# Retention heads: chunks of 128 tokens with carried states, and state products inside the head's last projection

## The chip, the cores and the metric

The kernel runs on one NeuronCore of one Trainium2 chip. The metric is device time in microseconds (us), of which less is better. Engines are named as in the profile: PE is TensorE's matmul side and PEld its weight load, DVE is VectorE, ACT is ScalarE, POOL is GpSimd, SP is SyncE, which here only issues DMAs. "L936" is line 936 of the kernel.

## What is computed

One step of a one-layer decoder whose mixer has two halves, eight heads of sparse attention and eight heads of retention, for a prompt of 512 tokens and for 8 samples of one token each (520 columns in all). The retention half, cut to what matters:

```python
def ret_chunk(R, q, k, v, lg):                      # RET_CHUNK = 128, dk = dv = 128
    decay = where(i - j >= 0, exp((i - j) * lg), 0)
    inner = einsum('bhij,bjhe->bihe', einsum('bihd,bjhd->bhij', q, k) * decay, v)
    cross = einsum('bihd,bhde->bihe', q, R) * exp((i + 1) * lg)
    zeta  = exp((n - 1 - i) * lg)
    R_new = exp(n * lg) * R + einsum('bjhd,bjhe,jh->bhde', k, v, zeta)
    return R_new, inner + cross
# prompt: lax.scan over 4 chunks from R = 0; samples: one step from a given state (8 x 8 x 128 x 128)
# then ret_o * rsqrt(mean(ret_o^2) + eps) * silu(gate), next to the attention half, @ w_out, MLP
```

Outputs are the two results, the new keys and values, and the retention states of the prompt and of the samples.

## The kernel before, in words

Activations lie in SBUF with features on partitions and the 520 tokens on the free side. Each projection is in "tiles": one tile makes 128 output features for 520 tokens, by two units of 8 contraction steps. Weights and activations are split into a high and a low part, so a step has three products (high by high, high by low, low by high), each for two halves of 260 tokens: 48 matmuls a unit, 96 a tile (`unit` and `tile`, L647). SP loads a unit's weights to one of two raw buffers, ACT makes the high part in a ring of four, POOL the low part from it.

The part that is changed is a loop over 8 heads. One round makes attention head i and retention head i. PE's order in a round is written out by hand: four tiles (values, queries, keys, gate of the retention head), and between their units or behind them the small products of both heads. All of these go through four PSUM banks `B`. The product groups of a round are numbered; `fill(e)` on PE waits until the group three before e has been taken out, DVE's `full(e)` waits until group e is there. DVE takes every group out, in order; the semaphore `s_xd` counts this.

In a round before the change:

- between the units of the second tile (`values_and_scores`): values turned, attention scores (groups 0 to 5)
- behind the third tile: the attention probabilities turned (groups 6 to 9)
- between the units of the fourth tile (`output_and_decay`): the attention output (group 10), the retention scores of each block of 128 keys with all later queries, 512, 384, 256 and 128 columns (groups 11 to 14, from `rk` and `rq`), the keys turned (15 and 16). DVE multiplies the scores by the decay `dh` to `sd_h` (L1713), makes `ktok` (turned keys by zeta, L1716), `ks_tok` and `vbd` (samples' keys and values in split form, L1657 to L1719)
- behind the fourth tile, "the tail": samples' key-value products (17 and 18, which DVE adds to the decayed states `rs`, L1725), the retention output from `sd_h` and `vtok_r` by 512, 384, 256 and 128 columns (19), the prompt's state from `ktok` and `vtok_r` (20), the samples' outputs, eight products of one column with `rs` (21). DVE copies the output to `ro`, ACT squares it to `rv`, PE sums the squares with a matrix `ones` (22 for the prompt, 23 for the samples), DVE takes the sums out.

Then DVE and ACT form the root, its inverse (L1432 to L1436) and the gated product into `mix` (L1741), beside the next round's first tile. SP waits for this before it loads the next `dh`, `rs` and a weight unit. In the last round ACT also copies `mix` to the input of the output projection (`mixed`, L1156), before and between its squares; POOL (L605) and DVE (L1747) form the low parts, step by step as that projection asks for them.

The core of the code before, in the tail:

Of the kernel before, what the change touches and what calls it, by code (L numbers as in the profile page):

```python
# [14 lines left out]
P = 128  # L15
D = 2048
KT = D // P
NP_, NS = 512, 8
T = NP_ + NS
# [42 lines left out]
def unit_of(tile):  # L62

    return 2 * tile
# [59 lines left out]
def build(nc, x_prompt, x_sample, cache_k, cache_v, cache_idx_k, state_ret, page_table, norm1_g, w_in,  # L124
# [3 lines left out]
    with ctx:  # L128
# [109 lines left out]
        sd_h = at("sd_h", H0, [P, 1280])  # L238
# [90 lines left out]
        def pos_stored(pos):  # L329
# [24 lines left out]
         s_th, s_hs, s_head) = (  # L354
# [4 lines left out]
                "ret_sqrt", "head_done"))  # L359
# [275 lines left out]
        def _(pe):  # L635
# [192 lines left out]
            with pe.Fori(0, NH) as i:  # L828
                m0, n0 = TILE_HEAD + 4 * i, unit_of(TILE_HEAD) + 8 * i

                e0 = 24 * i

                def head_tile(u, between=None):
                    tile(m0 + u, TILE_HEAD + u, n0 + 2 * u, unit_of(TILE_HEAD) + 2 * u, between=between)

                def fill(e):

                    pe.wait_ge(s_xd, e0 + TAKEN0 + max(e - 3, 0))
                    return e % 4

                def values_and_scores():
                    pe.wait_ge(s_evac, m0 + 1)
                    pe.wait_ge(s_head, i + 1)
                    x = fill(0)
                    for k in range(QB):
                        last = turn(B[:, x, k * P:(k + 1) * P], rv[:, k * P:(k + 1) * P], P)
                    last.then_inc(s_xp, 1)  # L850
                    turn(B[0:NS, fill(1), 0:P], rv[:, NP_:T], P).then_inc(s_xp, 1)
                    pe.wait_ge(s_qc, i + 1)
                    for b in range(QB):
                        mm(B[:, fill(2 + b), 0:P * (b + 1)], qc[:, b * P:(b + 1) * P], kt[:, 0:P * (b + 1)]
                           ).then_inc(s_xp, 1)

                def output_and_decay():
                    x = fill(10)
                    pe.wait_ge(s_xd, e0 + TAKEN0 + 10)
                    for k in range(QB):  # L860
                        last = mm(B[:, x, k * P:NP_], vtok[:, k, :], pt_h[:, KOFF[k]:KOFF[k] + NP_ - k * P],
                                  start=(k == 0), stop=(k == QB - 1))
                    last.then_inc(s_xp, 1)
                    pe.wait_ge(s_rk, i + 1)
                    for k in range(QB):
                        mm(B[:, fill(11 + k), 0:NP_ - k * P], rk[:, k * P:(k + 1) * P], rq[:, k * P:NP_]
                           ).then_inc(s_xp, 1)
                    x = fill(15)
                    for k in range(QB):
                        last = turn(B[:, x, k * P:(k + 1) * P], rk[:, k * P:(k + 1) * P], P)  # L870
                    last.then_inc(s_xp, 1)
                    turn(B[0:NS, fill(16), 0:P], rk[:, NP_:T], P).then_inc(s_xp, 1)
# [191 lines left out]
        def _(act):  # L1064
# [93 lines left out]
            def act_head(i, last=False):  # L1158
# [29 lines left out]
                act.wait_ge(s_xd, 24 * i + TAKEN0 + 20)  # L1188
                act_fn(rv[:, 0:NP_], ro[:, 0:NP_], ACT.Square).then_inc(s_sq, 1)
                act.wait_ge(s_xd, 24 * i + TAKEN0 + 22)  # L1190
# [6 lines left out]
                act.wait_ge(s_xd, 24 * i + TAKEN0 + 24)  # L1197
# [228 lines left out]
        def _(dve):  # L1426
# [239 lines left out]
            with step.loop(NH, 14) as i:  # L1666
                m0, e0 = TILE_HEAD + 4 * i, 24 * i
# [17 lines left out]
                step(v.tensor_copy(st[:, 41:42], gamma[:, one(i)]))  # L1685
                v.tensor_copy(qc[:, :], row(qa, i)[:, 0:NP_]).then_inc(s_qc, 1)
# [29 lines left out]
                v.tensor_tensor(ktok[:, :, :], B[:, full(15), :].rearrange("p (k d) -> p k d", d=P),  # L1716
                                st[:, 37:41].unsqueeze(2).to_broadcast([P, QB, P]), ALU.mult).then_inc(s_xd, 1)
                split_thirds(ks_tok, B[0:NS, full(16), 0:P], ("hi", "hi", "lo")).then_inc(s_xd, 1)
# [12 lines left out]
                for n, cols in enumerate((slice(0, NP_), slice(NP_, T))):  # L1731
                    v.tensor_scalar(rv[:, cols], B[:, full(22 + n), 0:cols.stop - cols.start], 1.0 / P, EPS,
                                    ALU.mult, ALU.add).then_inc(s_xd, 1)
# [381 lines left out]
```

## Time and profile before

| what | value |
|---|---|
| median of 3 runs | 2383.7 us (2379.57 to 2384.89) |
| profiled execution: its own time | 2381.4 us |
| profiled execution: span from first to last instruction | 2379.6 us |
| mean granted TensorE clock | 0.989 |
| busy: PE, PEld, DVE, ACT, POOL | 97%, 94%, 68%, 38%, 36% |
| loop over heads | about 324 to 822 us of the span, 62.1 us a round |

The loop is a fifth of the span. Its rounds are alike, so one can be read for all; the fourth (511.6 to 573.5 us) is used, and the last separately, because what follows it is different. Times in the rows are from the span's start. One matmul of the code appears in the trace as two records of PE, each with a weight load. A PE record lasts longer than the distance to the next one, since they are pipelined; what a group costs is read from the start of its first record to the start of the next group.

### The profile page before, as it was taken

What the parts mean: (1) busy time and instruction counts of PE and PEld (TensorE: products, weight loads), DVE (VectorE), ACT (ScalarE), POOL (GpSimd) and SP (SyncE); (2) the same over time, 40 slices, a digit from 0 to 9 for tenths busy, and PEclk for the clock granted to TensorE, in tenths of its full rate; (3) what the DMA queues carried; (4) which work ended last, traced back from release to release, by engine and by line L of the source; (5) the groups of instructions that cost most, each with busy time, mean ns of one, the idle gap of its engine ahead of it and who ended that gap; (6) DMA issues with size and microseconds to landing.
All of it is one profiled execution on the core that took longest, in us unless ns stands there. A gap on an engine that the chain in (4) does not pass through costs nothing.

```text
span 2379.6 us, 46108 instructions
## 1 busy us (share of the span) xinstructions
PE 2319.0 (97%) x18386; PEld 2244.1 (94%) x18386; DVE 1620.7 (68%) x2452; ACT 912.4 (38%) x1180; POOL 854.7 (36%) x355
## 2 busy tenths in 40 slices
PE   8999999999999999999999999999899999999997
PEld 7979899999999899989999999999899999999996
DVE  5358725555555533478888899888877777777775
ACT  5241222222222433355555555555433333333344
POOL 2522322232333444333333333333333333333354
PEclk9999999999999999999999999999999999999998
DMA  6533323333333353425555555566875567655621
GB/s 222 131 80 91 95 63 86 94 85 94 83 81 86 103 178 115 129 74 185 201 199 187 188 191 185 189 201 201 300 256 199 189 210 246 209 185 197 225 97 72
DMA packets 349079, 368.77 MB, mean 155 GB/s; under 512 B 16818, under 2 KB 301682, under 8 KB 348018
## 3 DMA queue, kind: packets, MB, share of 16 engines
q1 hardware_dynamic: 336866, 352.16, 46.5%
q10 hardware_dynamic: 12064, 14.53, 1.7%
q8 instruction: 105, 1.72, 0.3%
q14 instruction: 44, 0.36, 0.1%
HBM read 288.85 MB, written 77.80 MB: 154 GB/s over the span
## 4 chain that ended last, share of the span: by engine, by line
PE 67%; DVE 20%; issue 7%; ACT 4%; DMA 1%; POOL 0%; ACTq 0%; SPq 0%; DVEq 0%; POOLq 0%
PE product L647 30%; PE product L936 29%; DVE banks L1867 7%; PE banks L678 6%; DVE h_lo L1908 4%; ACT w_hi L1249 3%; DVE h_f L1897 2%; DVE w_lo L1873 2%; PE banks L675 1%; DVE c_b L1832 1%; DMA x_in<-in_x_prompt_dram 1%; DVE h_f L1899 1%; DMA w_raw<-in_w_in_dram 1%; ACT h_f L1073 1%; DVE a_lo L1456 0%
## 5 line engine op out<-in xcount | busy, mean ns | idle before, releaser
L615 POOL TENSOR_TENSOR w_lo<-raw,w_hi 128x1024 fp32r<-128x1024 f32 x193 | 495.2, 2566 | 825.5 <-ACT w_hi L1249 825.3
L936 PE MATMUL product<-s_up,w_hi 128*128 128x260 f32 x3600 | 657.4, 284 | 9.0 <-DVE w_lo L1873 5.4
L936 PE MATMUL product<-s_dn,w_hi 128*128 128x260 f32 x3584 | 652.4, 284 | 8.8 <-DVE xr L1975 3.3
L936 PEld LDWEIGHTS product<-s_up,w_hi 128*128 128x128 f32 x3600 | 557.1, 189 | 15.2 <-DVE w_lo L1873 10.5
L936 PEld LDWEIGHTS product<-s_dn,w_hi 128*128 128x128 f32 x3584 | 552.6, 188 | 12.7 <-issue 4.9
L582 POOL TENSOR_TENSOR w_lo<-w_raw,w_hi 128x1024 fp32r<-128x1024 f32 (+1 forms) x134 | 321.8, 2404 | 659.2 <-ACT w_hi L1070 659.0
L936 PE MATMUL product<-s_up,w_lo 128*128 128x260 f32 x1800 | 510.1, 283 | 0.0
L936 PE MATMUL product<-s_dn,w_lo 128*128 128x260 f32 x1792 | 506.9, 283 | 0.0
L647 PE MATMUL product<-a_hi,w_hi 128*128 128x260 f32 (+1 forms) x2144 | 439.6, 286 | 8.9 <-DVE a_lo L1456 3.9
L647 PE MATMUL product<-a_hi,w_lo 128*128 128x260 f32 (+1 forms) x2144 | 433.5, 284 | 0.0
L647 PE MATMUL product<-a_lo,w_hi 128*128 128x260 f32 (+1 forms) x2144 | 432.7, 283 | 0.0
L1249 ACT CAST w_hi<-banks 128x1024 fp32r<-128x1024 f32 x244 | 247.1, 1013 | 452.4 <-DVE banks L1867 342.4
L1873 DVE TENSOR_TENSOR w_lo<-banks,w_hi 128x1024 fp32r<-128x1024 f32 x244 | 297.9, 1221 | 105.5 <-ACT w_hi L1249 105.5
L1070 ACT CAST w_hi<-w_raw 128x1024 fp32r<-128x1024 f32 (+1 forms) x134 | 139.6, 1043 | 555.7 <-PE product L647 414.7
L647 PEld LDWEIGHTS product<-a_hi,w_hi 128*128 128x128 f32 (+1 forms) x2144 | 331.4, 189 | 16.5 <-issue 8.1
L936 PEld LDWEIGHTS product<-s_up,w_lo 128*128 128x128 f32 x1800 | 340.2, 189 | 0.0
L936 PEld LDWEIGHTS product<-s_dn,w_lo 128*128 128x128 f32 x1792 | 336.8, 188 | 0.0
L647 PEld LDWEIGHTS product<-a_hi,w_lo 128*128 128x128 f32 (+1 forms) x2144 | 331.4, 189 | 0.0
L647 PEld LDWEIGHTS product<-a_lo,w_hi 128*128 128x128 f32 (+1 forms) x2144 | 330.3, 188 | 0.0
L1249 ACT CAST w_hi<-raw 128x1024 fp32r<-128x1024 f32 x193 | 203.2, 1053 | 187.5 <-PE product L936 170.3
L1975 DVE TENSOR_TENSOR xr<-xr,product 128x260 f32<-128x260 f32 x416 | 174.5, 420 | 122.7 <-PE product L936 121.2
L1867 DVE TENSOR_TENSOR banks<-raw 128x1024 f32<-128x1024 f32 x118 | 191.9, 1626 | 0.0
(289 smaller groups left out, 1875.6 us busy)
## 6 DMA issues: line engine op xcount, KB each, us to landing
raw<-in_w_up_dram SPq DMA_DIRECT2D x64, 1024.0 KB, 8.4
raw<-in_w_down_dram SPq DMA_DIRECT2D x64, 1024.0 KB, 5.7
s_dn<-hidden_combinations SPq DMA_DIRECT2D x112, 520.0 KB, 8.5
w_raw<-in_w_in_dram SPq DMA_DIRECT2D x100, 512.0 KB, 3.9
hidden_combinations<-h_hi SPq DMA_DIRECT2D x31, 910.0 KB, 3.8
hidden_combinations<-h_lo SPq DMA_DIRECT2D x31, 910.0 KB, 6.6
w_raw<-in_w_out_dram SPq DMA_DIRECT2D x32, 512.0 KB, 4.0
x_transposed<-xr ACTq DMA_DIRECT2D x2, 2080.0 KB, 7.6
```

The costliest lines, as they stand in the source:

```text
L582: nc.gpsimd.tensor_tensor(w_lo[:, slot, :, 0:cols], w_raw[:, raw, :, 0:cols], w_hi[:, slot, :, 0:cols].bitcast(F32), ALU.subtract).then_in ...
L615: nc.gpsimd.tensor_tensor(ring(w_lo, g, n), block_of(g, i, j), ring(w_hi, g, n).bitcast(F32), ALU.subtract).then_inc(s_lo, 1)
L647: last_mm = nc.tensor.matmul(out[:, half, :], w[:, slot, k, 0:cols], a[:, k0 + k, half * HT:(half + 1) * HT], start=(first and k == 0 and ...
L678: return nc.tensor.matmul(out, lhsT, rhs, start=start, stop=stop, skip_group_check=True)
L936: mm_last = nc.tensor.matmul(out, w[:, k, col:col + P], s[:, h, k, :], start=(first and k == 0 and part == 0), stop=(last and k == kn - 1 ...
L1070: nc.scalar.copy(w_hi[:, n % RING, :, 0:cols], w_raw[:, n % 2, :, 0:cols]).then_inc(s_hi, 1)
L1249: nc.scalar.copy(ring(w_hi, g, n), x).then_inc(s_hi, 1)
L1867: v.tensor_tensor(out, x, y, ALU.add).then_inc(s_t, 1)
L1873: v.tensor_tensor(ring(w_lo, g, n), sums_in(g, (k + 1) % 2), ring(w_hi, g, n).bitcast(F32), ALU.subtract).then_inc(s_lt, 1)
L1897: v.tensor_tensor(h_f[:, 5, :], h_f[:, 0, :], a21[:, :], ALU.subtract)
L1908: v.tensor_tensor(low[:, :, :], h_f[:, :, :], high[:, :, :].bitcast(F32), ALU.subtract).then_inc(s_hl, 1)
L1975: ins = v.tensor_tensor(acc, acc, part, op)
```

## The change

Scores of retention are made within a chunk of 128 tokens only (group 11, one bank: four products of 128 columns), and one DVE instruction multiplies them by the decay. The state at the end of each chunk is carried: PE makes the four partial states into the four quarters of one bank (group 14), DVE carries them on by the decay of a chunk (`carry`, three of them; the fourth step gives the prompt's state `rst`), and the retention output has, beside the product within the chunk, one with the carried state and decayed queries `rqd` (group 17). The partial states and the samples' key-value products (groups 15 and 16) are issued inside the second unit of the fourth tile, ahead of its seventh step (`partial_states`, at k = 14). DVE takes the gate tile out (`rg`) after the states in place of before them. The sum of the samples' squares goes to free columns of the bank of the samples' output, with semaphores of its own. A round has 20 groups where it had 24.

```diff
-        sd_h = at("sd_h", H0, [P, 1280])
+        sd_h = at("sd_h", H0, [P, NP_])
+        carry = at("carry", H0 + 2048, [P, QB - 1, P])
+        rqd = at("rqd", H0 + 3584, [P, NP_ - P])
...
 (PE, output_and_decay)
                     pe.wait_ge(s_rk, i + 1)
+                    x = fill(11)
                     for k in range(QB):
-                        mm(B[:, fill(11 + k), 0:NP_ - k * P], rk[:, k * P:(k + 1) * P], rq[:, k * P:NP_]
-                           ).then_inc(s_xp, 1)
-                    x = fill(15)
+                        last = mm(B[:, x, k * P:(k + 1) * P], rk[:, k * P:(k + 1) * P], rq[:, k * P:(k + 1) * P])
+                    last.then_inc(s_xp, 1)
+                    x = fill(12)
...
+                def partial_states(k):
+                    if k != 14:
+                        return
+                    x = fill(14)
+                    pe.wait_ge(s_xd, e0 + TAKEN0 + 14)
+                    for c in range(QB):
+                        last = mm(B[:, x, c * P:(c + 1) * P], ktok[:, c, :], vtok_r[:, c, :])
+                    last.then_inc(s_xp, 1)
+                    pe.wait_ge(s_vbd, i + 1)
+                    for j in range(2):
+                        mm(B[:, fill(15 + j), :], ks_tok[:, :], vbd[:, 4 * j:4 * j + 4, :]).then_inc(s_xp, 1)
...
-                head_tile(3, between=output_and_decay)
-                pe.wait_ge(s_vbd, i + 1)
-                for j in range(2):
-                    x = fill(17 + j)
-                    pe.wait_ge(s_xd, e0 + TAKEN0 + 17)
-                    mm(B[:, x, :], ks_tok[:, :], vbd[:, 4 * j:4 * j + 4, :]).then_inc(s_xp, 1)
-                x = fill(19)
+                head_tile(3, between=output_and_decay, ready=partial_states)
+                x = fill(17)
                 for k in range(QB):
-                    last = mm(B[:, x, k * P:NP_], vtok_r[:, k, :], sd_h[:, KOFF[k]:KOFF[k] + NP_ - k * P],
-                              start=(k == 0), stop=(k == QB - 1))
+                    out = B[:, x, k * P:(k + 1) * P]
+                    last = mm(out, vtok_r[:, k, :], sd_h[:, k * P:(k + 1) * P], stop=(k == 0))
+                    if k:
+                        if k == 1:
+                            pe.wait_ge(s_cq, i + 1)
+                        pe.wait_ge(s_sc1, 3 * i + k)
+                        last = mm(out, carry[:, k - 1, :], rqd[:, (k - 1) * P:k * P], start=False)
                 last.then_inc(s_xp, 1)
-                x = fill(20)
-                for k in range(QB):
-                    last = mm(B[:, x, 0:P], ktok[:, k, :], vtok_r[:, k, :], start=(k == 0), stop=(k == QB - 1))
-                last.then_inc(s_xp, 1)
-                x = fill(21)
-                pe.wait_ge(s_xd, e0 + TAKEN0 + 19)
+                x = fill(18)
+                pe.wait_ge(s_xd, e0 + TAKEN0 + 17)
                 for b in range(NS):
                     last = mm(B[:, x, b:b + 1], rs[:, b, :], rq[:, NP_ + b:NP_ + b + 1])
                 last.then_inc(s_xp, 1)
-                for n, cols in enumerate((slice(0, NP_), slice(NP_, T))):
-                    pe.wait_ge(s_sq, 2 * i + 1 + n)
-                    mm(B[:, fill(22 + n), 0:cols.stop - cols.start], ones[:, :], rv[:, cols]).then_inc(s_xp, 1)
+                pe.wait_ge(s_sq, 2 * i + 1)
+                mm(B[:, fill(19), :], ones[:, :], rv[:, 0:NP_]).then_inc(s_xp, 1)
+                pe.wait_ge(s_sq, 2 * i + 2)
+                mm(B[:, x, NS:2 * NS], ones[:, :], rv[:, NP_:T]).then_inc(s_vs, 1)
...
 (ACT: the squares wait for groups 17 and 18 in place of 19 and 21; the root waits for both sums)
...
 (DVE)
+                step(v.reciprocal(st[:, 45:46], st[:, 37:38]))
...
-                for k in range(QB):
-                    n = NP_ - k * P
-                    v.tensor_tensor(sd_h[:, KOFF[k]:KOFF[k] + n], B[:, full(11 + k), 0:n], dh[:, 0:n], ALU.mult
-                                    ).then_inc(s_xd, 1)
+                v.tensor_tensor(sd_h[:, :].rearrange("p (k d) -> p k d", d=P),
+                                B[:, full(11), :].rearrange("p (k d) -> p k d", d=P),
+                                dh[:, 0:P].unsqueeze(1).to_broadcast([P, QB, P]), ALU.mult).then_inc(s_xd, 1)
...
-                scaled(halves(rg[:, :]), m0 + 3, (TILE_HEAD + 1) % 2)
+                v.tensor_tensor(rqd[:, :], rq[:, P:NP_], dh[:, P:NP_], ALU.mult).then_inc(s_cq, 1)
+                x = full(14)
+                v.tensor_scalar(carry[:, 0, :], B[:, x, 0:P], st[:, 45:46], None, ALU.mult).then_inc(s_sc1, 1)
+                for k in range(1, QB - 1):
+                    dve.wait_ge(s_sc1, 3 * i + k)
+                    v.scalar_tensor_tensor(out=carry[:, k, :], in0=B[:, x, k * P:(k + 1) * P], scalar=st[:, 45:46],
+                                           in1=carry[:, k - 1, :], op0=ALU.mult, op1=ALU.add).then_inc(s_sc1, 1)
+                dve.wait_ge(s_sc1, 3 * i + 3)
+                v.scalar_tensor_tensor(out=rst[:, :], in0=carry[:, QB - 2, :], scalar=st[:, 37:38],
+                                       in1=B[:, x, (QB - 1) * P:NP_], op0=ALU.mult, op1=ALU.add).then_inc(s_xd, 1)
                 dve.wait_ge(s_rs, 16 * i + 16)
                 for j in range(2):
                     r4 = rs[:, 4 * j:4 * j + 4, :]
                     v.scalar_tensor_tensor(out=r4, in0=r4, scalar=st[:, 41:42],
-                                           in1=B[:, full(17 + j), :].rearrange("p (b e) -> p b e", e=P),
+                                           in1=B[:, full(15 + j), :].rearrange("p (b e) -> p b e", e=P),
                                            op0=ALU.mult, op1=ALU.add).then_inc(s_xd, 1)
-                v.tensor_copy(ro[:, 0:NP_], B[:, full(19), :]).then_inc(s_xd, 1)
-                v.tensor_copy(rst[:, :], B[:, full(20), 0:P]).then_inc(s_xd, 1)
-                v.tensor_copy(ro[:, NP_:T], B[:, full(21), 0:NS]).then_inc(s_xd, 1)
+                scaled(halves(rg[:, :]), m0 + 3, (TILE_HEAD + 1) % 2)
+                v.tensor_copy(ro[:, 0:NP_], B[:, full(17), :]).then_inc(s_xd, 1)
+                x = full(18)
+                v.tensor_copy(ro[:, NP_:T], B[:, x, 0:NS]).then_inc(s_xd, 1)
```

## Rows read from the trace of the kernel before

**Rows 1.** The page: the chain that ended last, share of the span by engine.
```profile
PE 67%; DVE 20%; issue 7%; ACT 4%; DMA 1%; POOL 0%; ACTq 0%; SPq 0%; DVEq 0%; POOLq 0%
```

**Rows 2.** The chain in order of time, heads' loop: start us, us, what.
```profile
511.57 17.57 PE product L647 x144
...
567.11 6.28 PE banks L678 x38
...
573.46 19.06 PE product L647 x144
...
833.98 8.15 DVE a_lo L1747 x6
```

**Rows 3.** PE's timeline between the units of the fourth tile: start us, us, what.
```profile
556.30 2.32 PE L678 MATMUL banks<-pt_h,vtok 128*128 128x512 f32 x8
558.46 2.32 PE L678 MATMUL banks<-rq,rk 128*128 128x512 f32 x8
...
561.08 0.49 PE L647 MATMUL product<-a_hi,w_hi 128*128 128x260 f32 x2
```

**Rows 4.** PE's timeline of the same round's tail, and the next tile's start.
```profile
566.95 0.62 PE L678 MATMUL banks<-vbd,ks_tok 72*128 72x512 f32 x2
567.40 2.32 PE L678 MATMUL banks<-sd_h,vtok_r 128*128 128x512 f32 x8
569.56 1.06 PE L678 MATMUL banks<-vtok_r,ktok 128*128 128x128 f32 x8
570.45 1.84 PE L678 MATMUL banks<-rq,rs 128*128 128x1 f32 x16
572.16 1.23 PE L678 MATMUL banks<-rv,ones 128*128 128x512 f32 x4
573.46 0.50 PE L647 MATMUL product<-a_hi,w_hi 128*128 128x260 f32 x2
```

**Rows 5.** PEld's timeline of the same tail; in brackets idle time before and releaser.
```profile
567.84 0.19 PEld L678 LDWEIGHTS banks<-sd_h,vtok_r 128*128 128x128 f32 x1 [0.24 <-issue]
...
572.87 0.42 PEld L678 LDWEIGHTS banks<-rv,ones 128*128 128x128 f32 x2 [0.43 <-DVE ro L1730]
```

**Rows 6.** DVE's timeline of the fourth round, and the end of its epilogue.
```profile
531.14 0.29 DVE L1693 SCALAR_TENSOR_TENSOR p_h<-banks,const 128x128 f32<-128x128 f32 x1
...
559.52 1.73 DVE L1713 TENSOR_TENSOR sd_h<-banks,dh 128x512 f32<-128x512 f32 x4
561.26 0.69 DVE L1716 TENSOR_TENSOR ktok<-banks,st 128x512 f32<-128x512 f32 x1
...
562.77 1.22 DVE L1719 TENSOR_TENSOR vbd<-vs_tok,const 72x1024 fp32r<-72x1024 f32 x1
...
567.76 1.40 DVE L1725 SCALAR_TENSOR_TENSOR rs<-rs,st,banks 128x512 f32<-128x512 f32 x2
569.76 0.69 DVE L1728 COPY ro<-banks 128x512 f32<-128x512 f32 x1 [0.60 <-PE banks L678]
...
572.33 0.17 DVE L1730 COPY ro<-banks 128x8 f32<-128x8 f32 x1 [1.39 <-PE banks L678]
...
582.62 2.63 DVE L1741 SCALAR_TENSOR_TENSOR mix<-rk,rg 128x520 f32 x1 [0.17 <-DVE rk L1740]
```

**Rows 7.** ACT's timeline of the fourth round's tail.
```profile
570.49 0.63 ACT L1073 ACTIVATE rv<-ro 128x512 f32<-128x512 f32 x1 [1.76 <-DVE ro L1728]
572.53 0.21 ACT L1073 ACTIVATE rv<-ro 128x8 f32<-128x8 f32 x1 [1.42 <-DVE ro L1730]
```

**Rows 8.** ACT's timeline of the last round's tail.
```profile
816.23 1.05 ACT L1070 CAST w_hi<-w_raw 128x1024 fp32r<-128x1024 f32 x1 [9.59 <-PE product L647]
...
819.82 0.63 ACT L1073 ACTIVATE rv<-ro 128x512 f32<-128x512 f32 x1
821.57 0.21 ACT L1073 ACTIVATE rv<-ro 128x8 f32<-128x8 f32 x1 [1.12 <-DVE ro L1730]
```

**Rows 9.** Stretch behind a tail: busy PE, PEld, DVE, ACT, POOL; granted clock; DMA.
```profile
573.46:577.00 3.54, 3.54 (x18) 3.54 (x19) 2.58 (x4) 3.20 (x3) 0.00 (x0) 0.56 0.53 167
```

More of the change, by code:

```diff
@@ L353, in build @@
         (s_qc, s_swap, s_rq, s_rk, s_xp, s_xd, s_nm, s_exp, s_pn, s_dh, s_rs, s_rst, s_rso, s_vbd, s_sq,
-         s_th, s_hs, s_head) = (
+         s_th, s_hs, s_head, s_cq, s_sc1, s_vs, s_vt) = (
             sem(n) for n in (
@@ L358, in build @@
                 "sample_state_stored", "values_diagonal", "ret_squared", "gate_tanh",
-                "ret_sqrt", "head_done"))
+                "ret_sqrt", "head_done", "ret_q_decayed", "states_carried", "sample_squares", "sample_var"))
         (s_t1h, s_t1p, s_t1, s_xb, s_n2, s_n2m, s_n2v, s_n2s, s_nf, s_nfm, s_nfv, s_nfs, s_yt,
@@ L829, in _, with head_tile @@
                 m0, n0 = TILE_HEAD + 4 * i, unit_of(TILE_HEAD) + 8 * i
-                e0 = 24 * i
-                def head_tile(u, between=None):
-                    tile(m0 + u, TILE_HEAD + u, n0 + 2 * u, unit_of(TILE_HEAD) + 2 * u, between=between)
+                e0 = 20 * i
+                def head_tile(u, between=None, ready=None):
+                    tile(m0 + u, TILE_HEAD + u, n0 + 2 * u, unit_of(TILE_HEAD) + 2 * u, between=between,
+                         ready=ready)
                 def fill(e):
@@ L871, in output_and_decay @@
                     last.then_inc(s_xp, 1)
-                    turn(B[0:NS, fill(16), 0:P], rk[:, NP_:T], P).then_inc(s_xp, 1)
+                    turn(B[0:NS, fill(13), 0:P], rk[:, NP_:T], P).then_inc(s_xp, 1)
+                def partial_states(k):
[9 more added lines that the diff above has]
+                        mm(B[:, fill(15 + j), :], ks_tok[:, :], vbd[:, 4 * j:4 * j + 4, :]).then_inc(s_xp, 1)
                 head_tile(0)
@@ L1187, in act_head @@
                     mixed(0, 4)
-                act.wait_ge(s_xd, 24 * i + TAKEN0 + 20)
+                act.wait_ge(s_xd, 20 * i + TAKEN0 + 18)
                 act_fn(rv[:, 0:NP_], ro[:, 0:NP_], ACT.Square).then_inc(s_sq, 1)
-                act.wait_ge(s_xd, 24 * i + TAKEN0 + 22)
+                act.wait_ge(s_xd, 20 * i + TAKEN0 + 19)
                 act_fn(rv[:, NP_:T], ro[:, NP_:T], ACT.Square).then_inc(s_sq, 1)
@@ L1196, in act_head @@
                     mixed(4, 5)
-                act.wait_ge(s_xd, 24 * i + TAKEN0 + 24)
+                act.wait_ge(s_xd, 20 * i + TAKEN0 + 20)
+                act.wait_ge(s_vt, i + 1)
                 act_fn(rk[:, :], rv[:, :], ACT.Sqrt).then_inc(s_hs, 1)
@@ L1664, in _ @@
             step(v.memset(vs_tok[:, :].bitcast(F32), 0.0))
-            with step.loop(NH, 14) as i:
-                m0, e0 = TILE_HEAD + 4 * i, 24 * i
+            with step.loop(NH, 15) as i:
+                m0, e0 = TILE_HEAD + 4 * i, 20 * i
                 def full(e):
@@ L1710, in _ @@
                 dve.wait_ge(s_dh, 16 * i + 16)
-                for k in range(QB):
-                    n = NP_ - k * P
-                    v.tensor_tensor(sd_h[:, KOFF[k]:KOFF[k] + n], B[:, full(11 + k), 0:n], dh[:, 0:n], ALU.mult
-                                    ).then_inc(s_xd, 1)
+                v.tensor_tensor(sd_h[:, :].rearrange("p (k d) -> p k d", d=P),
+                                B[:, full(11), :].rearrange("p (k d) -> p k d", d=P),
+                                dh[:, 0:P].unsqueeze(1).to_broadcast([P, QB, P]), ALU.mult).then_inc(s_xd, 1)
                 dve.wait_ge(s_rst, 16 * i + 16)
-                v.tensor_tensor(ktok[:, :, :], B[:, full(15), :].rearrange("p (k d) -> p k d", d=P),
+                v.tensor_tensor(ktok[:, :, :], B[:, full(12), :].rearrange("p (k d) -> p k d", d=P),
                                 st[:, 37:41].unsqueeze(2).to_broadcast([P, QB, P]), ALU.mult).then_inc(s_xd, 1)
-                split_thirds(ks_tok, B[0:NS, full(16), 0:P], ("hi", "hi", "lo")).then_inc(s_xd, 1)
+                split_thirds(ks_tok, B[0:NS, full(13), 0:P], ("hi", "hi", "lo")).then_inc(s_xd, 1)
                 v.tensor_tensor(vbd[:, :, :], vs_tok[:, :].bitcast(F32).unsqueeze(1).to_broadcast([K3, NS, P]),
                                 ident3.unsqueeze(2).to_broadcast([K3, NS, P]), ALU.mult).then_inc(s_vbd, 1)
-                scaled(halves(rg[:, :]), m0 + 3, (TILE_HEAD + 1) % 2)
+                v.tensor_tensor(rqd[:, :], rq[:, P:NP_], dh[:, P:NP_], ALU.mult).then_inc(s_cq, 1)
[8 more added lines that the diff above has]
+                                       in1=B[:, x, (QB - 1) * P:NP_], op0=ALU.mult, op1=ALU.add).then_inc(s_xd, 1)
                 dve.wait_ge(s_rs, 16 * i + 16)
@@ L1725, in _ @@
                     v.scalar_tensor_tensor(out=r4, in0=r4, scalar=st[:, 41:42],
-                                           in1=B[:, full(17 + j), :].rearrange("p (b e) -> p b e", e=P),
+                                           in1=B[:, full(15 + j), :].rearrange("p (b e) -> p b e", e=P),
                                            op0=ALU.mult, op1=ALU.add).then_inc(s_xd, 1)
-                v.tensor_copy(ro[:, 0:NP_], B[:, full(19), :]).then_inc(s_xd, 1)
-                v.tensor_copy(rst[:, :], B[:, full(20), 0:P]).then_inc(s_xd, 1)
-                v.tensor_copy(ro[:, NP_:T], B[:, full(21), 0:NS]).then_inc(s_xd, 1)
-                for n, cols in enumerate((slice(0, NP_), slice(NP_, T))):
-                    v.tensor_scalar(rv[:, cols], B[:, full(22 + n), 0:cols.stop - cols.start], 1.0 / P, EPS,
-                                    ALU.mult, ALU.add).then_inc(s_xd, 1)
+                scaled(halves(rg[:, :]), m0 + 3, (TILE_HEAD + 1) % 2)
+                v.tensor_copy(ro[:, 0:NP_], B[:, full(17), :]).then_inc(s_xd, 1)
+                x = full(18)
+                v.tensor_copy(ro[:, NP_:T], B[:, x, 0:NS]).then_inc(s_xd, 1)
+                v.tensor_scalar(rv[:, 0:NP_], B[:, full(19), :], 1.0 / P, EPS, ALU.mult, ALU.add).then_inc(s_xd, 1)
+                dve.wait_ge(s_vs, i + 1)
+                v.tensor_scalar(rv[:, NP_:T], B[:, x, NS:2 * NS], 1.0 / P, EPS, ALU.mult, ALU.add).then_inc(s_vt, 1)
                 dve.wait_ge(s_th, i + 1)
```

## The prediction

> **What bounds the kernel now.** I read the page first. The chain that ended last is mostly PE [rows 1]. Then the chain of waits in order of time through the loop over heads: from the first to the last tail it is PE alone, piece by piece without a gap worth naming, 62.1 us a round. A round is 17 to 19 us of tiles, small products, tiles again, and a tail of 6.3 us of products in the banks [rows 2]. So what a round costs is what PE has to issue, plus short waits in the tail. DVE and ACT matter only where PE waits for them. This is why the timelines of PE come next, between the units of the fourth tile [rows 3] and in the tail [rows 4], and then those of the weight load, DVE and ACT around the tail [rows 5 to 7], to find what PE waits for now and what it would wait for next. Behind the last tail the chain goes over to DVE's low parts [rows 2], so the last round is costed apart.
>
> **The retention scores.** The attention output (four products of 512, 384, 256 and 128 columns, eight records) takes 558.46 - 556.30 = 2.16 us [rows 3]. The retention scores have the same shapes, so 2.16 us as well. After the change they are four products of 128 columns. The trace has these too, the prompt's state: eight records from 569.56 to 570.45, 0.89 us, 0.111 us each [rows 4]. Saved: 2.16 - 0.89 = 1.27 us a round.
>
> **The retention output.** Before, 569.56 - 567.40 = 2.16 us [rows 4]. After, four products of 128 columns within the chunk and three with the carried state: fourteen records, 14 x 0.111 = 1.55 us. Saved: 0.61 us.
>
> The price of 0.111 us for such a record is what everything hangs on. From below, 2.16 us for 1280 columns is 0.216 us for 128 columns of a product, 0.108 us a record. From above stands the duration of a weight load, 0.19 us [rows 5], if loads didn't overlap, and 0.19 + 0.11 = 0.30 us, if nothing did. I take 0.111: the state's eight records have a load each, accumulate in one bank, and have exactly these shapes. The Trainium skill (TensorE: Matmul & The Clock Gate, Back-to-back issue gap) gives a sustained 81 ns for a matmul of 128 columns with its load, and 131 ns for 512 columns: narrow products would cost 0.62 of a wide one. A record of 512 columns takes 0.427 us here, so a narrow one would be 0.265 us, an estimate from that page, and the two edits would together lose 22 x 0.265 - 4.32 = 1.5 us a round, in place of gaining 1.9. The trace's 0.111 disagrees with it by far.
>
> **The partial states and the samples' products, moved into the tile.** They are the same instructions: 0.89 us for the states, and 567.40 - 566.95 = 0.45 us for the two with `vbd` [rows 4]. Moved, they gain nothing in PE's own time. They cost one more return from small products to a tile: 0 to 0.25 us, since the first pair behind such a return lasts 0.49 us [rows 3] where a pair of a tile takes 2 x 17.57/144 = 0.24 us [rows 2]. I take 0.1.
>
> Does PE wait there? It returns to the tile at 561.08 - 1.27 = 559.8. A unit takes 566.95 - 561.08 = 5.87 us, six of its eight steps 4.40, so it comes to `partial_states` at 564.2. DVE has to be through with `ks_tok` by then. It takes the attention output out until 559.5 as before, multiplies the scores in one instruction of 0.69 us where it had four of 1.73 together, and goes on with `ktok`, `ks_tok` and `vbd` [rows 6] about 1.0 us earlier: `ks_tok` is there at 561.8 and `vbd` (before 562.77 + 1.22 = 563.99) at 563.0. `vbd` is wanted at 564.2 + 0.9 = 565.1. Cover: 2.4 and 2.1 us. `rqd`, 384 columns, is new: 0.3 to 1.2 us by the nearest rows (128x128 and 72x1024 [rows 6]), I take 0.55, ready at 563.6, wanted at 567.5.
>
> The tile then ends at 559.8 + 5.87 + 1.34 + 0.1 = 567.1, where it was 566.95: the 1.27 us saved are what pays for the moved work.
>
> **The tail.** DVE gets the partial states at 564.2 + 0.9 + 0.2 = 565.3. Four dependent steps of 128 columns, 0.29 us each [rows 6] and 0.04 between, make the carried states until 566.3 and `rst` until 566.6. PE wants the first at 567.5 and the last at 568.4: no wait. The samples' states are 1.40 us more, to 568.0; `rg` to 568.7. PE is through with the output at 567.1 + 1.55 = 568.67, DVE copies it (0.69 [rows 6]) 568.9 to 569.6, ACT squares it (0.63 [rows 7]) to 570.2. Meanwhile PE has the samples' outputs, 572.16 - 570.45 = 1.71 us [rows 4], until 570.4. The sum of squares can start at once: 2 x 0.427 = 0.85, to 571.25. The samples' column: copied 570.6 to 570.8, squared (0.21) to 571.0, ready before 571.25. So the last product needs no wait and the next tile starts at about 571.5. Before, the dense sum ended at 572.16 + 0.85 = 573.01 and the next tile began at 573.46; the weight load waited 0.43 us, for the samples' square [rows 4, 5, 7]. Of these 0.45 some 0.2 are the eight-column product and 0.2 to 0.25 the wait. I take 0.15 as saved. If DVE's copy is late instead, up to 0.5 us is lost each round; it is the first thing to be late here, since the copy and the square fill just the 1.7 us of the samples' outputs.
>
> **Sum of a round:** 1.27 + 0.61 - 0.10 + 0.15 = 1.93 us. Seven rounds: 13.5 us.
>
> **The last round.** The input of the output projection is paced by POOL at first and then by DVE's low parts [rows 2], which wait for this head's result. ACT's order is cast of the weights (816.23), tanh, four casts, square (819.82), samples' square (821.57) [rows 8]. Tanh now waits for `rg`, so the square starts 0.4 to 0.5 us later, but the samples' square stands right behind it in place of 821.57: 0.6 us earlier from the tile's end, which is itself 0.15 later. The result comes some 0.3 us earlier, between -1 (DVE instructions that collide with POOL's) and +1. Taken: 0.3.
>
> **Off the path.** DVE gets one reciprocal, `rqd`, and four short steps for one copy. Even in the tail it stands idle ahead of PE's groups, 0.60 and 1.39 us [rows 6], so its own work isn't the limit. SP's queue is passed by nothing: the loads of `dh`, `rs` and weights wait for the same head's end, which moves with the round.
>
> **Total:** 13.5 + 0.3 = 13.8 us of the profiled execution's 2381.4: 2367.6. The median shown is 2.3 above it, so against the median it is 2383.7 - 13.8 = 2369.9; I give 2369.
>
> **Rivals.**
>
> *Narrow products cost more than 0.111 us (ends slower).* In place of 2.16 + 2.16 = 4.32 us, 22 records. At the weight load's 0.19 us they take 4.18: with the other terms 0.2 us a round is left, 2382, no change. Both edits together are even at 4.32/22 = 0.196 us; at 0.30 us they take 6.6, 2.3 us more, less 0.05: 18 us, 2402. For it: in the output the operands alternate between `vtok_r` with `sd_h` and `carry` with `rqd`, which no row shows. Against it: the state's row. At no change 0.04, slower 0.03. The rival with the page's 0.265 us would give some 12 us more, 2396, and is within these.
>
> *A wait inside the tile.* PE stands at k = 14 for `ks_tok` or `vbd`. DVE instructions with two SBUF operands can be held, as 2.63 us of `mix` where others of the kind take 0.7 [rows 6]. A hold of 1.9 us on `vbd` is within the cover of 2.1. It would have to be 4 us to eat the gain, each round. Chance 0.06, a third of it slower: with a wait of 1 us, 8 us lost, 2377.
>
> *The clock.* Behind one tail the granted clock is 0.56 over 3.5 us: mostly 1.2 GHz where the rest of the loop has 2.4 [rows 9]. What PE did before it: sixteen records of one column, a short sum, a wait [rows 4]. The tiles after it took 19.06 where they take 17.57: 1.5 us a fall [rows 2]. There is one in eight rounds. The change leaves the one-column records as they are and shortens the wait; the falls may go (-1.5) or be two or three (+1.5 to +3). A fall in each of the eight would cost 7 x 1.5 = 10.5 and leave 3: 2380, no change. Chance of five or more falls 0.04.
>
> **How the numbers follow.** The forecast has 0.83. Its own range: savings of 9 (half a microsecond of wait in a few tails, two more falls) to 17 (no fall, a free return to the tile), 2366 to 2375, and 2 or 3 us for the medians. That is 2363 to 2377. It takes in small waits in the tile; the rest is outside it. A change of this kernel's time can be told from none at about 0.2%, 4.8 us. Faster: the forecast, and part of the waits: 0.86. Within 0.2%: 0.08. Slower: 0.06.
>
> **What would show it.** In the changed kernel's profile: a round of 60.1 us; the group of scores 0.89 us; the output's fourteen records 1.55 us; no idle PE or weight load ahead of the states; DVE's `carry` ended before the gate tile; the sum of squares right behind the samples' outputs. Wrong, if the fourteen records take over 2 us, if the tile ends much later than it did, or if `ro` is copied so late that PE stands ahead of the sum.

## The result and the profile after

The median is 2366.5 us over 6 runs (2363.0 to 2373.8), against 2381.9 before over 6 runs (the three of the table before, with a median of 2383.7, and three more). The ratio is 0.9937, with a 95% interval of 0.9926 to 0.9947: faster by 15 us, between 13 and 18, where 14 to 15 were forecast. The profiled execution took 2368.2 us, with a span of 2366.4, 13.2 less than before. One of the six executions of a kernel below ("k = 15, wide") took 3823 us, at a mean granted clock of 0.62, and is left out of its median.

The chain in order of time through a round and into the next, of the kernel after (start us, us, what), answers to [rows 2]:

```profile
506.79 17.54 PE product L649 x144
...
551.65 3.05 PE banks L680 x16
...
555.24 4.34 PE product L649 x36
559.58 1.35 PE banks L680 x10
560.93 1.44 PE product L649 x12
562.37 4.33 PE banks L680 x34
566.70 17.54 PE product L649 x144
...
626.62 19.04 PE product L649 x144
```

It is still PE alone. A round is 566.70 - 506.79 = 59.91 us, where it was 573.46 - 511.57 = 61.89. The tail is 4.33 us where it was 6.28; the last unit of the fourth tile is cut in two by a piece of 1.35 us; the piece in the middle of that tile, with the attention output and the scores, is 3.05 us. The pieces marked x144 are the first of a round, one tile and a half. (That a matmul of the code is two records holds for the products in the banks only: in the tiles 48 matmuls are 48 records.) Three of these pieces, at 626.62 and twice more, take 19.04 to 19.06 in place of 17.54 us, as one did before.

PE's timeline of the same round (start us, us, what), which answers to [rows 3, 4]:

```profile
553.64 1.06 PE L680 MATMUL banks<-rq,rk 128*128 128x128 f32 x8
554.53 0.71 PE L677 MATMUL banks<-const,rk 128*128 128x128 f32 x5
555.00 0.49 PE L649 MATMUL product<-a_hi,w_hi 128*128 128x260 f32 x2
...
559.41 1.05 PE L680 MATMUL banks<-vtok_r,ktok 128*128 128x128 f32 x8
560.22 0.71 PE L680 MATMUL banks<-vbd,ks_tok 72*128 72x512 f32 x2
560.77 0.40 PE L649 MATMUL product<-a_hi,w_hi 128*128 128x260 f32 x2
...
562.21 0.60 PE L680 MATMUL banks<-sd_h,vtok_r 128*128 128x128 f32 x4
562.65 0.39 PE L680 MATMUL banks<-rqd,carry 128*128 128x128 f32 x2
562.88 0.39 PE L680 MATMUL banks<-sd_h,vtok_r 128*128 128x128 f32 x2
...
563.77 1.84 PE L680 MATMUL banks<-rq,rs 128*128 128x1 f32 x16
565.47 1.23 PE L680 MATMUL banks<-rv,ones 128*128 128x512 f32 x4
566.67 0.50 PE L649 MATMUL product<-a_hi,w_hi 128*128 128x260 f32 x2
```

The scores take 554.53 - 553.64 = 0.89 us. The records that alternate between `sd_h` and `carry` start 0.23 us a pair apart (562.65, 562.88), and the fourteen take 563.77 - 562.21 = 1.56. DVE's timeline shows the row behind the moved products, and how little room it has (start us, us, what, idle before and releaser):

```profile
557.99 0.55 DVE L1735 TENSOR_TENSOR rqd<-rq,dh 128x384 f32<-128x384 f32 x1
560.51 0.35 DVE L1737 TENSOR_SCALAR carry<-banks,st 128x128 f32<-128x128 f32 x1 [1.97 <-PE banks L680]
560.89 0.74 DVE L1740 SCALAR_TENSOR_TENSOR carry<-banks,st,carry 128x128 f32<-128x128 f32 x2
561.67 0.35 DVE L1743 SCALAR_TENSOR_TENSOR rst<-carry,st,banks 128x128 f32<-128x128 f32 x1
561.93 1.40 DVE L1748 SCALAR_TENSOR_TENSOR rs<-rs,st,banks 128x512 f32<-128x512 f32 x2
563.25 0.69 DVE L1490 TENSOR_TENSOR rg<-product,rb 128x520 f32<-128x520 f32 x1
563.97 0.69 DVE L1752 COPY ro<-banks 128x512 f32<-128x512 f32 x1
```

The gate tile is out at 563.94 and the copy of the output starts at 563.97, just when PE's output is there: the two arrive together.

### The profile page after: what moved, and what is told of

Same layout as the page of the kernel before. It is cut to its first block, busy times and chain, and to the rows that moved or that the text cites. A ratio compares the mean times of both kernels' runs of the same rounds, so it can differ in the third digit from the quotient of the medians.

```text
span 2366.4 us, 46212 instructions
## 1 busy us (share of the span) xinstructions
PE 2306.1 (97%) x18434; PEld 2244.3 (95%) x18434; DVE 1628.1 (69%) x2468; ACT 912.1 (39%) x1180; POOL 852.9 (36%) x355
## 4 chain that ended last, share of the span: by engine, by line
PE 65%; DVE 21%; issue 7%; ACT 5%; DMA 1%; POOL 0%; DVEq 0%; ACTq 0%; SPq 0%; POOLq 0%
PE product L649 30%; PE product L949 28%; DVE banks L1891 7%; PE banks L680 5%; DVE h_lo L1932 4%; ACT w_hi L1263 3%; DVE w_lo L1897 2%; DVE h_f L1921 2%; PE banks L677 1%; DVE c_b L1856 1%; DMA w_raw<-in_w_in_dram 1%; DVE h_f L1923 1%; DMA x_in<-in_x_prompt_dram 1%; ACT h_f L1086 1%; DVE s_up L1838 1%
```

## The experiments

"Clean" is a round in which no tile shows a granted clock of 1.2 GHz; rounds are read in each chain of waits, from one round's first tile to the next's, in the one profile of each kernel. Ratios are to the kernel before, run beside each kernel.

| kernel | clean round us | rounds 2 to 7 that were longer | median us | ratio (95%) |
|---|---|---|---|---|
| before | 61.9 | 1 | 2381.9 | 1 |
| changed | 59.9 | 2 | 2366.5 | 0.9937 (0.9926 to 0.9947) |
| changed, once more | 59.9 | 0 | 2366.3 | 0.9945 (0.9928 to 0.9963) |
| placement alone | 61.8 | 0 | 2382.2 | 1.0003 (0.9994 to 1.0012) |
| placement undone | 61.1 in the wide form | all | 2384.3 | 1.0010 (1.0000 to 1.0019) |
| k = 8 | 62.2 | 2 | 2389.0 | 1.0032 (1.0021 to 1.0043) |
| k = 15 | 60.4 | 5 | 2379.2 | 0.9989 (0.9980 to 0.9998) |
| wide samples' outputs | 59.95 | 0 | 2369.2 | 0.9936 (0.9923 to 0.9949) |
| other order in last round | 59.9 | 0 | 2370.0 | 0.9951 (0.9938 to 0.9964) |
| both | 59.95 | 0 | 2363.2 | 0.9926 (0.9913 to 0.9938) |
| k = 15, wide | 60.4 | 0 | 2369.3 | 0.9964 (0.9951 to 0.9976) |
| placement undone, wide | 61.1 | 1 | 2376.0 | 0.9980 (0.9972 to 0.9989) |
| k = 12, both | 59.9 | 0 | 2364.9 | 0.9932 (0.9919 to 0.9945) |

### The placement alone

```diff
 (the kernel before; PE)
+                def state_and_samples(k):
+                    if k != 14:
+                        return
+                    x = fill(17)
+                    pe.wait_ge(s_xd, e0 + TAKEN0 + 17)
+                    (the four products of the state, then the two with vbd)
-                head_tile(3, between=output_and_decay)
+                head_tile(3, between=output_and_decay, ready=state_and_samples)
```

> The kernel before with the placement alone: the state (one sum of four products, 128 columns) and the samples' two products are issued ahead of the seventh step of the fourth tile's second unit; scores and output stay 512, 384, 256 and 128 columns wide. Theory (the narrow products give the gain, the placement moves work without removing any): a round stays at 61.9 us within 0.1, the time at 2382, within 3 of before. Rival (the placement gives a part, since the tail gets shorter): the tail shrinks by more than the tile grows, a round of 61.0 or less, 2375 or less.

A round is 61.8 us (391.76 to 453.56) and the ratio 1.0003. PE's timeline of its tail (start us, us, what), the tile having ended at 448.45:

```profile
448.45 2.32 PE L678 MATMUL banks<-sd_h,vtok_r 128*128 128x512 f32 x8
450.61 1.84 PE L678 MATMUL banks<-rq,rs 128*128 128x1 f32 x16
452.31 1.23 PE L678 MATMUL banks<-rv,ones 128*128 128x512 f32 x4
```

The tail is 1.4 us shorter than in [rows 4] (5.11 where it was 6.51), and the unit of the tile 1.3 us longer. Moving PE's work without removing any is worth 0.1 us a round.

### The placement undone

```diff
 (the changed kernel; PE)
-                head_tile(3, between=output_and_decay, ready=partial_states)
+                head_tile(3, between=output_and_decay)
+                partial_states(14)
 (DVE: the gate tile taken out ahead of the partial states, as before the change)
```

> The changed kernel with the placement undone: partial states and samples' products behind the fourth tile, the gate tile taken out by DVE before them as it was before the change; chunks and carried states stay. Theory (the placement is the cover for DVE's chain from the partial states over the carried ones and the samples' states to the samples' outputs): PE stands 1.0 to 1.3 us ahead of the samples' outputs, since DVE's four short steps and the 1.4 us for the samples' states come first; a round of 60.9 to 61.2 in place of 59.9, 2374 to 2376. Rival (narrow products are all, the placement is worth nothing): 59.9 a round and 2366.

The wait came out nearly as expected, the time did not: 2384.3, no faster than before the change. PE's timeline of a tail (start us, us, what, idle before and releaser):

```profile
508.96 0.39 PE L680 MATMUL banks<-sd_h,vtok_r 128*128 128x128 f32 x2
509.19 0.39 PE L680 MATMUL banks<-rqd,carry 128*128 128x128 f32 x2
510.47 1.95 PE L680 MATMUL banks<-rq,rs 128*128 128x1 f32 x16 [0.89 <-DVE rs L1750]
512.27 1.23 PE L680 MATMUL banks<-rv,ones 128*128 128x512 f32 x4
```

The samples' outputs wait for the samples' states, which DVE makes behind the carried ones: PE stands 0.89 us in every tail. Six rounds of this kernel take 63.40, 61.74, 62.59, 63.42, 61.74 and 62.51 us. The stretches of 3.64 us behind its tails say why (busy PE, PEld, DVE, ACT, POOL; granted clock; DMA share, GB/s):

```profile
388.36:392.00 3.64, 3.64 (x17) 3.64 (x18) 2.13 (x4) 2.88 (x3) 0.00 (x0) 0.53 0.51 162
451.76:455.40 3.64, 3.64 (x25) 3.64 (x26) 2.14 (x4) 2.96 (x3) 0.00 (x0) 0.78 0.42 135
513.50:517.14 3.64, 3.64 (x30) 3.64 (x31) 2.14 (x4) 2.85 (x3) 0.00 (x0) 1.00 0.51 162
576.09:579.73 3.64, 3.64 (x18) 3.64 (x18) 2.14 (x4) 2.96 (x3) 0.00 (x0) 0.51 0.36 115
```

The clock fell to 1.2 GHz in or behind five of the seven tails between rounds, as it did once in [rows 9]. This is the cost that I had put at chance for the changed kernel.

### Where in the tile: k = 8 and k = 15

```diff
 (the changed kernel, PE)
-                    if k != 14:
+                    if k != 8:          (and, in another kernel, 15)
```

> The changed kernel with the partial states six steps earlier, at k = 8, the first step of the second unit. Theory (the cover that I computed for k = 14): PE stands 1.9 us for the samples' split keys (ready 1.85 us after the tile's return) and 0.3 us for vbd, 2.2 us a round, so all of the gain is gone: round of 62.1, 2383. Rival (DVE gets through earlier if asked earlier, or PE's wait is made up in the tail because all that follows on DVE is early): 60 to 61 a round, under 2375.

> The changed kernel with the partial states one step later, at k = 15, 0.73 us. Theory (behind the tile DVE's carried states, samples' states, gate tile and copy of the output stand in one row that is just in time at k = 14): the copy of the output starts 0.7 us later, and the sum of squares with it, since PE's samples' outputs cover only what they cover now: 0.5 to 0.7 us a round, 60.5, 2370 to 2372. Rival (there is slack in this row): 59.9, 2366.

At k = 8 PE waits, as the cover computed for k = 14 says it must (PE's timeline, start us, us, what, idle before and releaser):

```profile
504.12 1.16 PE L680 MATMUL banks<-vtok_r,ktok 128*128 128x128 f32 x8 [1.63 <-DVE ks_tok L1674]
505.44 0.73 PE L680 MATMUL banks<-vbd,ks_tok 72*128 72x512 f32 x2 [0.17 <-DVE vbd L1733]
```

From start to start PE is 1.9 us late ahead of the states and 0.5 ahead of the products with `vbd`, where 1.9 and 0.3 were expected. The clean round is 62.2 (454.06 to 516.28), 2.3 over the changed kernel where 2.2 was expected; nothing of it is made up later. The time is 6 us above the 2383 expected. Two of the rounds take 63.8 with a fallen clock, 1.5 us each, and eight rounds of 2.3 are 18.5 us, not the 16.5 I had added; that is 5 of the 6.

At k = 15, one step later, the clean round is 60.4 (390.71 to 451.08), as expected. DVE's row starts 0.7 us later against the scores, the copy of the output 0.6. But two things are late then, and PE meets the samples' states first (PE's timeline, start us, us, what, idle before and releaser):

```profile
447.89 1.95 PE L680 MATMUL banks<-rq,rs 128*128 128x1 f32 x16 [0.15 <-DVE rs L1748]
449.84 1.24 PE L680 MATMUL banks<-rv,ones 128*128 128x512 f32 x4
```

The sum of squares then starts at 449.84, 0.13 us behind ACT's square of the copied output, which ends at 449.71. The samples' outputs take 1.95 us from their start to that of the sum, where they take 1.70 in the changed kernel and 1.80 behind the longer wait above, so the square is what held the sum last.

The time was 7 us above the upper end of the expectation, 2372. Five of the six rounds take longer, 60.8 to 62.5, together 5.7 us more than five clean ones.

### The samples' outputs 48 columns wide

```diff
 (PE)
-                    last = mm(B[:, x, b:b + 1], rs[:, b, :], rq[:, NP_ + b:NP_ + b + 1])
+                    last = mm(B[:, x, 16 + 48 * b:64 + 48 * b], rs[:, b, :], rq[:, T - 48:T])
 (DVE)
-                v.tensor_copy(ro[:, NP_:T], B[:, x, 0:NS]).then_inc(s_xd, 1)
+                v.tensor_copy(ro[:, NP_:T], B[:, x, 56:400:49]).then_inc(s_xd, 1)
```

On the changed kernel, beside a second run of it unaltered:

> The changed kernel once more, unaltered, as the base for the three that follow, and for another look at the granted clock. Theory (the stretch with 1.2 GHz behind a tail comes by chance and costs 1.5 us each time): clean rounds of 59.91 us again, rounds with a fall 61.4, but another number of falls than three. Rival (the falls belong to rounds 6 to 8 of this kernel): the same three. Time 2366, 2363 to 2374.

> The changed kernel with each of the samples' eight output products 48 columns wide in place of one; the column wanted is picked out of them by DVE. Theory A (the clock falls behind a tail because sixteen records of one column keep the array nearly idle for 1.7 us): a record stays 0.107 us, no stretch of 1.2 GHz within rounds 2 to 7, all rounds 59.9, 2361 to 2364, and less scatter. Theory B (the falls have another cause, the waits or chance): as many falls as without, one to three, 2366. Rival on the price: a 48-column record takes longer than 0.107, a round of over 60.5.

The unaltered kernel had no fall in rounds 2 to 7 this time, with 59.90 to 59.92 us each: the falls in its first profile were chance. The wide form had none either, so here it couldn't tell the theories apart. Its time, 2369.2, is above the 2361 to 2364 expected, and its interval overlaps that of the unaltered kernel: for the changed kernel a gain of the width is not shown. The two kernels whose rounds were mostly longer can tell more:

> The kernel with the partial states at k = 15, and each of the samples' eight output products 48 columns wide instead of one. Without the width its clean rounds were 60.4 us as expected, but the clock fell behind or in four tails of the loop, and the time was 2379 in place of 2371. Theory A (the sixteen records of one column leave the array nearly idle, and the waits ahead of and behind them make the stretch long enough for the clock to fall): with 48 columns no fall in rounds 2 to 7, 60.4 each, 2370 to 2372. Theory B (the falls come from the waits alone): as many falls as without, 2379.

> The kernel with the placement undone, and 48 columns in the samples' output products. Without the width the wait of 0.9 to 1.1 us ahead of them was as expected, but five of the seven rounds had a stretch of 1.2 GHz, and the time was 2384 in place of 2375. Theory A (the one-column records together with the wait): no fall or one, rounds of 61.0 to 61.2, 2375 to 2377; the placement is then worth some 9 us by its cover and the rest by keeping the clock up. Theory B (waits alone): 2384 again.

With 48 columns the kernel with k = 15 comes to 2369.3 (ratio 0.9964, against 0.9989) and all its rounds are 60.40 to 60.44. The five executions reach from 2365.9 to 2375.3, so this median is loose; the ratio would stand for some 2373. The one with the placement undone comes to 2376.0 (0.9980, against 1.0010). Its tail has the same wait, and a record costs hardly more than with one column (PE's timeline, start us, us, what, idle before and releaser):

```profile
509.70 1.99 PE L680 MATMUL banks<-rq,rs 128*128 128x48 f32 x16 [0.89 <-DVE rs L1750]
511.52 1.21 PE L680 MATMUL banks<-rv,ones 128*128 128x512 f32 x4
```

Behind it the clock stays at 2.4 GHz (columns as above):

```profile
390.52:394.16 3.64, 3.64 (x30) 3.64 (x31) 2.13 (x4) 2.92 (x3) 0.00 (x0) 1.00 0.51 162
451.63:455.27 3.64, 3.64 (x30) 3.64 (x31) 2.13 (x4) 2.86 (x3) 0.00 (x0) 1.00 0.51 162
512.74:516.38 3.64, 3.64 (x30) 3.64 (x31) 2.13 (x4) 2.86 (x3) 0.00 (x0) 1.00 0.51 162
573.84:577.48 3.64, 3.64 (x30) 3.64 (x31) 2.14 (x4) 2.86 (x3) 0.00 (x0) 1.00 0.51 162
```

The same wait of 0.89 us, wider records, and a fall at one of the seven tails between rounds, the last, in place of five. The executions without a kept trace say the same: with one column the mean granted clock of all eleven executions is 0.980 to 0.986, with 48 columns 0.986 to 0.990; at k = 15 it is 0.983 to 0.987, and 0.986 to 0.990 in the five. So in these two kernels most falls come with the sixteen records of one column together with the waits around them, and the waits alone are not enough for most. They can be enough: at the one tail with wide records where the clock fell, PE had stood the same 0.89 us. The Trainium skill (TensorE: Matmul & The Clock Gate, table "Why this matters for your kernels") names idle gaps of PE between bursts of matmuls as what makes the throughput drop. The traces agree that idle time matters and add that what PE does beside it does too: the same 0.89 us came with five falls beside one-column records and with one beside 48-column records.

### The last round

```diff
 (ACT, last round)
+                if last: mixed(0, 1)            (ahead of the tanh)
-                if last: mixed(0, 4)            (ahead of the squares)
-                if last: mixed(4, 5)
+                if last: mixed(1, 5)            (behind the squares)
```

> The changed kernel with another order on ACT in the last round: one cast of the attention output to the projection's input ahead of the tanh, the other four behind the squares, in place of four before the squares and one behind. Theory (in the last round PE stands 1.75 us ahead of the sum of squares because the square is queued behind tanh and four casts, and the clock falls on it): PE's idle time there is under 0.3 us, the result of the last head comes 1.5 to 2.5 us earlier, 2364. Rival (POOL's low parts, which need the casts, pace PE anyway): the idle time goes but the time stays at 2366.

> Wide samples' outputs and the other order of the last round together. Theory: the gains add, 2359 to 2362. Rival: neither is worth anything that lasts, 2366.

In the changed kernel PE stands still in the last tail, since the square is queued behind the tanh, which waits for the gate tile, and behind casts. PE's timeline of the unaltered kernel's second profile (start us, us, what, idle before and releaser):

```profile
804.22 1.84 PE L680 MATMUL banks<-rq,rs 128*128 128x1 f32 x16
807.82 2.30 PE L680 MATMUL banks<-rv,ones 128*128 128x512 f32 x4 [1.75 <-ACT rv L1086]
```

and of the one with the other order:

```profile
804.79 1.84 PE L680 MATMUL banks<-rq,rs 128*128 128x1 f32 x16
806.50 1.23 PE L680 MATMUL banks<-rv,ones 128*128 128x512 f32 x4
```

The idle time is gone. But `mix` is started 73.01 us after the round's start where it was 73.28: 0.27 us. DVE takes the sum out 2.85 us earlier against the round's start (807.64 - 747.82 = 59.82, where it was 809.92 - 747.25 = 62.67). Of this 1.57 is lost at once: the four casts that were ahead of the square are now ahead of the root, and DVE waits for the root (ACT's timeline, then DVE's):

```profile
807.83 2.20 ACT L1169 CAST a_hi<-mix 128x520 fp32r<-128x520 f32 x4 [0.75 <-issue]
812.09 3.40 DVE L1446 RECIPROCAL rk<-rk 128x520 f32<-128x520 f32 x1 [3.08 <-ACT rk L1086]
```

So the inverse of the root starts 1.28 us earlier (812.09 - 747.82 = 64.27, where it was 812.80 - 747.25 = 65.55), and 1.0 of that is given back in DVE's products with two SBUF operands, which take longer while POOL forms its low parts:

```profile
815.53 1.49 DVE L1447 TENSOR_TENSOR rq<-rv,rk 128x520 f32<-128x520 f32 x1
817.05 1.67 DVE L1448 TENSOR_TENSOR rq<-rq,rk 128x520 f32<-128x520 f32 x1
```

They are 0.70 us where POOL is idle. The rival of the expectation holds in what it says of the time, but not for its reason: the gain went to the moved casts and to DVE's instructions beside POOL's. The time, 2370.0, is even above the changed kernel's 2366.3, with overlapping intervals; the profiled execution spends 1538.0 us behind the loop (829.65 to its end at 2367.7), in code that is the same, where the unaltered kernel spends 1533.0 (829.32 to 2362.3). With the wide samples' outputs as well, the time is 2363.2, the lowest here, above the 2359 to 2362 expected, and its interval (0.9913 to 0.9938) overlaps that of the changed kernel: not shown to be faster.

### Two steps earlier, with both

> Wide samples' outputs, the other order on ACT in the last round, and the partial states two steps earlier, at k = 12. Theory (k = 14 is just in time for DVE behind the tile, and the cover ahead of it is over 1.5 us): no wait at k = 12 and none ahead of the copy of the output; clean rounds stay at 59.9, since the copy waits for PE's output products, 2361 to 2364. Rival (the earlier states shorten the tail's wait for the samples' square too): 59.5 or less a round, 2360 or less.

```diff
 (the kernel "both", PE)
-                    if k != 14:
+                    if k != 12:
```

The round is 59.94 (385.74 to 445.68) and the time 2364.9, a little above the 2361 to 2364 expected. There is no wait at k = 12, and none is saved in the tail, where the copy of the output waits for PE's products: the place between about k = 12 and 14 doesn't matter. The profile of this kernel has no fall in or behind any tail between rounds.

## Why the prediction was right

**What bounds.** Right: PE sets the round in both traces, and a round's change is PE's change.

**The scores and the output.** 1.27 us and 2.16 - 1.56 = 0.60 us, against 1.27 and 0.61. Records of 128 columns cost 0.111 us also when their operands alternate, so the rival of narrow products is refuted. The sum by the sustained figures of the Trainium skill (TensorE: Matmul & The Clock Gate, Back-to-back issue gap), a loss of 1.5 us a round, is refuted with it.

**The moved products.** From 555.00 to 562.21 the unit takes 7.21 us, 5.87 for itself and 1.34 for the moved products: the second return to the tile, for which I took 0.1, costs nothing. My bound of 0.25 for it set a duration, 0.49 us, against a distance, 0.24; a pair in the middle of a tile has a duration of 0.40 us too. The cover was as computed, within 0.2 us: at k = 8 PE is late by 1.9 and 0.5 us.

**The tail.** The wait saved is 0.10 us and not 0.15. The sum and what follows take 566.67 - 565.47 = 1.20 us, where [rows 4] have 1.30; the weight load still waits 0.36 us for the samples' square, where it waited 0.43 [rows 5]. The square is done 0.59 us behind the samples' outputs (0.6 in the forecast), but it was 0.58 before the change already (572.53 + 0.21 - 572.16), so the change moved nothing there, and my sentence that the last product needs no wait was wrong. What saves the 0.10 us is open. The sum of a round: 1.27 + 0.60 + 0.10 = 1.97, measured 61.89 - 59.91 = 1.98, forecast 1.93.

**The first thing to be late** was to be DVE's copy of the output. At k = 15 the square of this copy is what holds the sum of squares last, and a round costs 0.5 us more; but the samples' states come late as well, and PE stands 0.15 us for them first. I had given their lateness no place.

**The last round** was the wrong term. Forecast 0.3 us earlier; from the round's start to `mix` it was 833.37 - 760.61 = 72.76 us before and 820.53 - 747.25 = 73.28 in the second profile after: 0.5 later. I had seen the square come later behind tanh and casts, but let only the samples' square count. PE stands 1.75 us for the first square, so the sum starts no earlier in the round than before (807.82 - 747.25 = 60.57, where it was 821.19 - 760.61 = 60.58): all that the round had gained is waited away. The sum then takes 2.30 us instead of 1.23, at a fallen clock, and half of this loss comes back in DVE's products. The chain of waits in this tail goes over `carry`, the samples' states, the gate tile, tanh and casts.

**The clock.** One fall is 1.5 us, as taken (19.04 - 17.54). How many there are is chance in the changed kernel: three first tiles in one profile, none in another. The mechanism that I named, one-column records and a wait, is borne out by the wide forms for the two kernels that fall in most rounds, though one fall is left with wide records. In the changed kernel itself it is only argued. What the prediction lacked is that the clock depends on the placement. The clean rounds make the placement worth 61.1 - 59.9 = 1.2 us, some 9 us in all; the medians make it 2384.3 - 2366.5 = 17.8, and the rest is about the 8.3 us that the width alone gives back to the kernel with the placement undone (2384.3 - 2376.0).

**Luck.** Between rounds without a fall the change is worth 7 x 1.98 - 0.5 = 13.4 us, near the forecast sum of 13.8 because the round was a little better and the last round worse. The 13.2 us of the first pair of profiles agree with it by chance. From the loop's first tile to the output projection's first product, it is 518.0 us before (324.16 to 842.18) and 508.4 after (324.67 to 833.07), 9.6 less, with more falls after; another 4.1 us are gained behind that, where the code is the same. In the second profile, without a fall in those tails, it is 502.7, 15.3 less. Behind the loop the same code takes 1532 to 1538 us in the thirteen profiles, so differences of a few us between single executions say nothing.

**Where the gain comes from.** The two parts of the change need each other. Placement alone: 0.1 us a round. Chunks alone: 61.9 - 61.1 = 0.8. Together 2.0, because the chunks put 1.4 us of dependent DVE steps ahead of the 1.4 us for the samples' states, which only the placement hides.

## What to carry to other kernels

When an algorithm with less PE work brings a chain of small steps on another engine, find the tile of dense work that can hide the chain, and issue its first product as early as the inputs allow: here one step of 0.7 us too late costs 0.5 us a round and, in most rounds, a fallen clock besides. Where products of one column stand beside a wait and the clock falls there, try them wider: in two kernels here 48 columns cost the same and most falls went, while in a kernel with few falls nothing was gained for sure. A load or square that one stage queues behind casts for the next should be looked at again whenever the instruction ahead of it moves; and whoever moves the casts should look at what they stand ahead of next.

## What the runs showed of the hardware beyond that

Sixteen records of 48 columns take 1.82 us (511.52 - 509.70) and of one column 1.80 (512.27 - 510.47). With 48 the clock stayed at 2.4 GHz behind six of seven tails in which PE stood idle for 0.89 us; with one, it fell in or behind five of seven. A DVE product of 0.70 us with two SBUF operands took 1.49 and 1.67 us beside POOL's instructions.
